# A streaming encoder step on one core: the MLP joins the attention's block, its first falling weights are prepared in the mix, the second queries are fetched in the projection's end, and the input stage is put in another order

## The reference, cut to what matters

```python
p = rms_norm(x, g_pre_mix) @ w_in            # 1024 x 5064: queries, keys, values, index queries, gates
o_a = window attention (128 keys, sinks)     # 16 heads of 64
o_b = attention over the 256 keys that an indexer picks
x1  = x + rms_norm((sig(g_a)*o_a + sig(g_b)*o_b) @ w_o, g_post_mix)
hid = square(relu(rms_norm(x1, g_pre_mlp) @ w_up))          # 1024 -> 4096
y   = x1 + rms_norm(hid @ w_down, g_post_mlp)               # 4096 -> 1024
```

## Time and profile before

| | us |
|---|---|
| three runs | 1955.41, 1956.94, 1957.11 |
| median | 1956.94 |
| the profiled execution | 1953.25 |
| its span, first to last instruction | 1951.5 |
| PE busy in it | 1877.9 (96%) |
| DVE, ACT, POOL busy | 1148.3, 711.1, 601.5 |
| mean granted TensorE clock | 0.990 of full |

### The profile page before, as it was taken

How to read it: one execution, slowest core, us unless ns; L and a number is a source line. 1 busy time by engine, 2 the same in 40 slices (tenths; PEclk the granted TensorE clock), 3 DMA queues, 4 the chain that set the end, 5 groups by cost and what they waited for, 6 DMA issues and landing times. The chain is left out here.

```text
span 1951.5 us, 32608 instructions
## 1 busy us (share of the span) xinstructions
PE 1877.9 (96%) x11780; PEld 1775.0 (91%) x11780; DVE 1148.3 (59%) x2732; ACT 711.1 (36%) x1420; POOL 601.5 (31%) x460
## 2 busy tenths in 40 slices
PE   5999999999997999999999999999999999999995
PEld 5889999877777999999998879999999999999995
DVE  5249999998665666676764654334333343344346
ACT  4335544223334555555564332222222222222212
POOL 2316544234233444444332012222222222222214
PEclk9999999999998999999999999999999999999998
DMA  5423333233438444444223313111111111111204
GB/s 174 126 66 103 93 92 86 87 102 99 105 98 185 106 99 100 99 99 89 67 66 109 118 54 109 43 43 48 43 48 43 43 43 43 43 43 43 64 1 162
DMA packets 180396, 160.23 MB, mean 82 GB/s; under 512 B 101472, under 2 KB 148432, under 8 KB 180288
## 3 DMA queue, kind: packets, MB, share of 16 engines
q1 hardware_dynamic: 166144, 140.32, 25.4%
q10 hardware_dynamic: 14144, 18.49, 4.0%
HBM read 120.63 MB, written 39.27 MB: 82 GB/s over the span
## 5 line engine op out<-in xcount | busy, mean ns | idle before, releaser
L2264 PE MATMUL ps<-hid_hi,weights 128*128 128x362 f32 (+1 forms) x1536 | 381.7, 328 | 3.9 <-POOL weights L2124 3.9
L1726 PE MATMUL ps<-x2T_hi,weights 128*128 128x362 f32 (+1 forms) x1536 | 378.2, 326 | 1.8 <-POOL weights L1858 1.5
L2264 PEld LDWEIGHTS ps<-hid_hi,weights 128*128 128x128 f32 x1536 | 271.9, 189 | 4.2 <-POOL weights L2124 4.2
L1726 PEld LDWEIGHTS ps<-x2T_hi,weights 128*128 128x128 f32 x1536 | 272.1, 188 | 2.4 <-POOL weights L1858 1.7
L2203 DVE TENSOR_TENSOR total<-total,ps 128x364 f32<-128x364 f32 (+1 forms) x360 | 189.1, 532 | 139.9 <-PE ps L2264 139.9
L1726 PE MATMUL ps<-x2T_lo,weights 128*128 128x362 f32 (+1 forms) x768 | 251.4, 327 | 0.0
L2264 PE MATMUL ps<-hid_lo,weights 128*128 128x362 f32 (+1 forms) x768 | 251.1, 327 | 0.0
L974 PE MATMUL ps<-xT_hi,w 128*128 128x362 f32 (+1 forms) x960 | 245.0, 329 | 1.6 <-PEq L165 1.6
L2188 DVE TENSOR_TENSOR hidden<-hidden 128x362 f32<-128x362 f32 (+1 forms) x96 | 53.9, 562 | 296.9 <-ACT hidden L2162 296.9
L2124 POOL TENSOR_TENSOR weights<-down_raw,weights 128x512 fp32r<-128x512 f32 x64 | 83.4, 1304 | 406.4 <-ACT weights L2153 406.4
L950 DVE MATCH_REPLACE8 score<-top,score 128x1024 f32<-128x1024 f32 (+5 forms) x208 | 198.6, 960 | 0.0
(11 more groups left out here) (189 smaller groups left out, 3205.8 us busy)
## 6 DMA issues: line engine op xcount, KB each, us to landing
q_raw<-q_scr SPq DMA_DIRECT2D x80, 256.0 KB, 5.1
w_raw<-in_w_in ACTq DMA_DIRECT2D x64, 256.0 KB, 3.0
up_raw<-in_w_up SPq DMA_DIRECT2D x64, 256.0 KB, 2.8
down_raw<-in_w_down SPq DMA_DIRECT2D x64, 256.0 KB, 2.6
gates<-gate_scr SPq DMA_DIRECT2D x34, 256.0 KB, 4.8
x_in<-in_x_prompt SPq DMA_DIRECT2D x16, 512.0 KB, 4.8
gate_scr<-stage SPq DMA_DIRECT2D x32, 256.0 KB, 3.0
q_scr<-stage SPq DMA_DIRECT2D x40, 181.0 KB, 3.1
```

The lines of the kernel that those rows point to most:

```text
L1726: last = pe.matmul(ps[:, bank, 0:n], a[:, k, fs], b, start=(k == 0 and i == 0), stop=(k == KT - 1 and i == 2))
L2264: more = pe.matmul(ps[:, UP_BANKS + g % DOWN_BANKS, 0:n], a[:, f, cols], h, start=(f == 0 and i == 0), stop=(f == FT - 1 and i == 2))
```

## The change

**Input stage.** SP's order of loads becomes x0, gain, units 2 and 3, x1, units 4 and 5, x2, units 6 and 7, x3, and then one next-chunk unit and one x tile in turn, with the stores begun inside that loop. ACT's queue loads units 0 and 1 alone. Units 4 to 7 get buffers of their own (`w_more`), so no load of the first chunk waits. All hi copies are ACT's; DVE has none. ACT runs a one-column square root (`warm`) first. PE's order is turn(t), group(t-1). The next chunk's units are spread over the tiles.
**Projection's end.** The four mask stores go ahead of the store of group 6. The first part of the banded values stays on SP behind that store, the second part (7 DMAs) goes to ACT's queue behind its evacuation of group 7. `load_q(1)` moves to SP behind the store of group 7. On POOL, `split_queries(1)` comes first in the attention, with a wait for the projection's last group; the small memsets (`LATE_SETS`), on which SP's sample values wait, come behind it. SP's attention begins with the distances, then the values of the other branch, then the gates.
**The MLP.** It loses its block: its five programs run behind the mix's. Its first four falling units are loaded by SP in the mix (before the store of tile 7, behind the turn of the last merged tile), copied by ACT between the two statistics of the last tile, and subtracted by POOL behind the rising units. Its first rising group waits for each unit k when it needs it. The final waits of SP move to the end.

```diff
 @@ input_norm, SyncE
+load_x(0)
+sp.dma_start(gain[:], g_pre_mix[0:1, :].to_broadcast([P, D])).then_inc(gains_loaded, 16)
+load_first(2)
+load_first(3)
+load_x(1)
+load_first(4)
+load_first(5)
+load_x(2)
+load_first(6)
+load_first(7)
+load_x(3)
+for t in range(X_IN, TILES):
+    load_next(KT + t - X_IN)
+    load_x(t)
+    if t >= X_IN + 2:
+        store(t - X_IN - 2)
+for t in range(TILES - X_IN - 2, TILES):
+    if KT + t + 2 < 2 * KT:
+        load_next(KT + t + 2)
+    store(t)
 @@ input_norm, ScalarE
-for k in range(RAW):
-    load_weight_unit(act, ws, w_raw, w_in, k)
+for k in range(2):
+    load_first_unit(act, ws, k, as_loaded(k), w_in)
 act.wait_ge(const_ready, 1)
+act.activation(warm[:], c["eps"][:], ACT.Sqrt)
+for t in range(2):
+    mean_square(t)
+    weights_hi(2 * t)
+    weights_hi(2 * t + 1)
+for t in range(TILES):
+    split_hi(t)
+    if t < 2:
+        weights_hi(4 + 2 * t)
+        weights_hi(5 + 2 * t)
+    if t + 2 < TILES:
+        mean_square(t + 2)
+    if t >= 2:
+        evacuate(t - 2)
+    if KT <= KT + t - 1 < 2 * KT and t >= 1:
+        weights_hi(KT + t - 1)
 @@ input_norm, VectorE
-for k in range(HI_BY_DVE):
-    dve.wait_ge(ws["loaded"][k % RAW], weight_loads(k))
-    dve.tensor_copy(w_hi[:, half_of(0), k, 0:T_WIDTH], w_raw[:, k % RAW, 0:T_WIDTH]).then_inc(ws["hi_dve"], 1)
 @@ input_norm, TensorE
-for t in range(TILES + 2):
+for t in range(TILES + 1):
     if t < TILES:
         turn(t)
-    if t >= 2:
-        group(t - 2)
+    if t >= 1:
+        group(t - 1)
 @@ projection, SyncE, last chunk
+if ch == LAST and g == VALUES_AT:
+    store_last_masks()
 store(ch, g)
 if ch == LAST and g == VALUES_AT:
-    load_values(0)
-if ch == LAST and g == VALUES_AT + 1:
-    load_values(1)
+    load_values()
+if ch == LAST and g == SECOND_AT:
+    load_second_queries()
 @@ projection, ScalarE, last chunk
+if ch == LAST and g == SECOND_AT:
+    load_more_values()
 @@ attention, SyncE
-sp.wait_ge(kv["mask_ready"], MASKS)
-for n in range(MASKS - SCORES, MASKS):
...
+for i in range(2):
+    load_dist(i)
 for dst, src in B_VALUES:
     sp.dma_start(dst, src).then_inc(b_values_loaded, 16)
-for n in range(MASKS - SCORES, MASKS):
-    sp.wait_ge(mask_stored[mask_slot(n)], 16 * (n // SCORES + 1))
-load_q(1)
-for i in range(2):
-    load_dist(i)
 @@ attention, GpSimd
     if s >= 2:
         pool.wait_ge(scored, CHUNK_BASE[SECTION_END[s - 2]])
+    else:
+        pool.wait_ge(ws["group_done"], PROJECTED)
...
+split_queries(1)
 for u in range(PROJECTED - STAGE, PROJECTED):
     pool.wait_ge(ws["stored"][u % STAGE], stage_stores(u))
 @@ output_mix, SyncE
+if t == TILES - 2:
+    sp.wait_ge(m_turned, 2 * TILES)
+    for u in range(DOWN_UNITS):
+        load_down_unit(sp, down, u, 0)
 sp.wait_ge(x1_ready, t + 1)
 @@ output_mix, GpSimd, behind the rising units
+for u in range(DOWN_UNITS):
+    pool.wait_ge(down["hi_done"], u + 1)
+    split_down_lo(pool, down, u)
 @@ output_mix, ScalarE
     norm_statistics(t - 1, 0, product(t - 1))
+    if t == TILES:
+        for u in range(DOWN_UNITS):
+            act.wait_ge(down["loaded"][u], 16)
+            split_down_hi(act, down, u)
 @@ early_up, TensorE
-pe.wait_ge(up["lo_done"], KT)
-up_product(pe, ps, x2T, up, g, EARLY_BANKS[g])
+up_product(pe, ps, x2T, up, g, EARLY_BANKS[g], weights_as_made=(g == 0))
 @@ up_product
+if weights_as_made:
+    pe.wait_ge(up["lo_done"], k + 1)
 @@ mlp, TensorE, first chunk
+pe.wait_ge(kv["mix_scaled"], TILES)
+pe.wait_ge(kv["x_lo_done"], 2 * TILES)
 @@ streaming_step
+raised = mlp(nc, top, c, x2T, ps, kv, up, down, a["g_post_mlp"], x1_scr, o["y_prompt"], o["y_sample"])
...
     mixed.tensor(pe)
+    raised.tensor(pe)
...
-mlp(nc, top, c, x2T, ps, weights, up, a["w_down"], a["g_post_mlp"], x1_scr, o["y_prompt"], o["y_sample"])
```

More of the change, by code:

```diff
@@ L2019, in mlp @@
         up_raw, up_loaded, up_src = up["raw"], up["loaded"], up["src"]
-        down_raw = sb("down_raw", [P, DOWN_UNITS, 512])
-        size = KT * CH
-        quarter = [weights[:, i * size:(i + 1) * size] for i in range(4)]
-        up_hi, up_lo = up["hi"], up["lo"]
-        down_hi, down_lo = (w.rearrange("p (k n) -> p k n", k=FT) for w in quarter[2:])
+        up_hi, up_lo, down_hi, down_lo = up["hi"], up["lo"], down["hi"], down["lo"]
+        x1_in = sb("x1_in", [P, 2, D])
         hidden = sb("hidden", [P, 2, 364])
@@ new lines, in gpsimd, with split_up_lo, all_down_lo @@
+        def gpsimd(pool):
+            def split_up_lo(j):
+                for k in range(KT):
+                    pool.wait_ge(up_hi_done, j * KT + (k + 1))
+                    pool.tensor_tensor(up_lo[:, k, :], up_raw[:, k // 2, k % 2, :], up_hi[:, k, :].bitcast(F32),
+                                       ALU.subtract).then_inc(up_lo_done, 1)
+            def all_down_lo(j):
+                for u in range(DOWN_UNITS):
+                    pool.wait_ge(down_hi_done, j * DOWN_UNITS + (u + 1))
+                    split_down_lo(pool, down, u)
+            with pool.Fori(0, N_CH - 1) as j:
+                split_up_lo(j + 1)
+                all_down_lo(j + 1)
+            pool.wait_ge(down_lo_done, N_CH * DOWN_UNITS)
+            for t in range(TILES):
+                r = tile_rows(t)
+                pool.wait_ge(scaled, t + 1)
+                pool.wait_ge(x1_loaded[t % 2], 16 * (t // 2 + 1))
+                pool.tensor_tensor(y[:r, t % 3, :], y[:r, t % 3, :], x1_in[:r, t % 2, :], ALU.add).then_inc(y_ready, 1)
+                pool.wait_ge(y_ready, t + 1)
@@ new lines, in scalar, with split_up_hi, chunk @@
+        def scalar(act):
+            def split_up_hi(j):
+                act.wait_ge(up_done, j * N_UP)
+                for k in range(KT):
+                    act.wait_ge(up_loaded[k // 2], (j + 1) * 16)
+                    act.activation(up_hi[:, k, :], up_raw[:, k // 2, k % 2, :], ACT.Copy).then_inc(up_hi_done, 1)
+            def chunk(j, first=False):
+                for g in range(N_UP + 1):
+                    if g < DOWN_UNITS and not first:
+                        act.wait_ge(down_done, j * N_DOWN)
+                        act.wait_ge(down_loaded[g], (j + 1) * 16)
+                        split_down_hi(act, down, g)
+                    if g < N_UP:
+                        n = UP_GROUPS[g][2]
+                        act.wait_ge(up_done, j * N_UP + (g + 1))
+                        if g >= 2:
+                            act.wait_ge(hid_lo_done, j * N_UP + (g - 1))
+                        elif not first:
+                            act.wait_ge(hid_lo_done, j * N_UP)
+                        act.activation(hidden[:, g % 2, 0:n], ps[:, up_bank(g, first), 0:n], ACT.Relu).then_inc(relu_done, 1)
+                    if g >= 1:
+                        f, t0, n = UP_GROUPS[g - 1]
+                        act.wait_ge(squared_done, j * N_UP + g)
+                        act.activation(hid_hi[:, f, t0:t0 + n], hidden[:, (g - 1) % 2, 0:n], ACT.Copy).then_inc(hid_hi_done, 1)
+            chunk(0, first=True)
+            with act.Fori(1, N_CH) as j:
+                split_up_hi(j)
+                chunk(j)
+            for t in range(TILES):
+                r = tile_rows(t)
+                act.wait_ge(y_turned, t + 1)
+                act.activation(squares[:r], y_banks(t), ACT.Square, accum_out=col["sum_sq"][:r, t:t + 1]).then_inc(sq_done, 1)
+                act.wait_ge(sq_done, t + 1)
+                act.activation(col["std"][:r, t:t + 1], col["sum_sq"][:r, t:t + 1], ACT.Sqrt, bias=c["eps"][:r, :],
+                               scale=1.0 / D).then_inc(std_ready, 1)
```

514 lines of the change are left out of this document (241 added, 273 removed).

## The result

The changed kernel takes 1938.9 us (median of 4 runs, 1937.0 to 1939.9), the kernel before 1956.4 beside it (4 runs, 1955.4 to 1957.1): ratio 0.9914, 95% interval 0.9903 to 0.9926. That is 17.5 us faster where 24.3 were forecast; 1938.9 lies inside the range, 6.3 us above the predicted time. The profiled execution took 1938.89 with a span of 1937.1, 14.4 us shorter than the span of before.

The account below looks back on a forecast made before the run. TensorE, busy 96% of the span, was taken as the bound, with its waits at three places to remove: 8.0 + 8.4 + 7.9 = 24.3 us, from the median 1956.94 to 1932.6 us; range 1925 to 1945.

Parts of the forecast that it names:

- the input stage: Kernel's start: first product group starts near 16.9 us instead of 25.88; gain 8.0 us, bounds 3 and 10.
- x1 as the deciding load: Input stage: the second tile decides when group 0 starts; x1 lands near 10 us, its `x_norm` is done at 14.8.
- rival (c): Input stage: loads sharing the DMA engines are the bound, not VectorE's queue; gain there 3 us, time 1937.6, chance 0.12.
- the MLP's start: Start of the MLP: waits for falling and rising weights and a half-clock stretch go; gain 7.9 us, or down to 6.
- the projection's end: Before attention section 1: the wait for second queries goes, less later values; net gain 8.4 us, bounds 4.7 and 9.8.
- I take 1.0: First value product, section 0: values delayed by the queries' 1 MB beside them cost 1.0 us, bounds 0 and 4.2.
- the 3.7 us of slack: Before section 1: second queries land at 582.7 and are split by 589.2, 3.7 us before they are needed.
- Rival (a): Projection's end gives its gain back, values and queries delaying each other; total gain 16.9 us, time 1940.0, chance 0.14.
- 0.5 us: Section 1's first six score matmuls: the slower run behind the idle gap goes, counted 0.5 us, bounds 0 to 0.9.
- The 8.9 us go: Between sections 0 and 1: TensorE's whole idle time for the second queries, 8.9 us, is gained.
- Rival (b): Section 0: GpSimd's split stops VectorE, 6.5 us of the middle gain go; time 1939.1, chance 0.04.
- Rival (d): ScalarE's last evacuation before attention is late behind seven value DMAs; slower kernel, 1962.7 at 5 us each, chance 0.02.

Follow-up runs that it names:

- experiment 2: The changed kernel with SyncE issuing the last four distance stores behind the eight value loads instead of ahead of them; 1937.3 us.
- experiment 5: The changed kernel with GpSimd's subtraction of the first queries waiting for VectorE's last mask but one; 1935.9 us (three runs).
- filled_gap: The changed kernel with 21 unused 128x208 products on TensorE ahead of the first value product's wait for the values; 1933.5 us.
- experiment 3: The change without its input stage (1943.4 us), without its second queries' part (1941.5 us), and the kernel before with the MLP's part alone (1945.3 us).
- mlp_part_alone: The kernel before with only the MLP's part of the change; 1945.3 us.
- 7: The changed kernel with distances and half the values on ScalarE ahead of group 7's evacuation, plus fillers (1930.5 us); also with further edits together (1929.7 us).
- all_four: The changed kernel with distances and half the values on ScalarE before group 7, GpSimd's subtraction behind the last mask but one, 12, 10 and 6 fillers; 1929.7 us.
- experiment 6: The changed kernel with 12 unused 128x512 products ahead of the first index scores, those of the sample tile; 1939.3 us.
- masks_on_act: The changed kernel with distances and half the values issued on ScalarE ahead of its evacuation of group 7, no fillers; 1935.7 us.
- no_input_part: The changed kernel with the input stage of the kernel before; 1943.4 us.
- masks_on_act_filled: The changed kernel with distances and half the values on ScalarE ahead of group 7's evacuation, 10 fillers before the first turn, 6 before the first value product; 1930.5 us.
- no_queries_part: The changed kernel with the projection's end of the kernel before; 1941.5 us.

## Why the prediction was right and wrong

**Right, the input stage** (8.0 against 7.3 at the stage's end). Group 0 behind the second tile, x1 as the deciding load, 2.0 us for a half-clock turn: all there. x1 was in ScalarE's hands at 10.05 and its root at 11.23, as reckoned; rival (c) did not occur. x1's `x_norm` ended at 15.41, not 14.8. What no term held is that some of this could be lost later, where TensorE next waits; by medians 4.5 us of it remain.

**Right, the MLP's start** (7.9 against 8.5 by profile). The waits for falling and rising weights are gone, the first falling stretch runs at full clock in 23.59 us, and ScalarE's late copies delayed nothing.

**Wrong, the projection's end** (8.4 against -0.7 by profile, some 3 by medians). Two steps failed.

The first is the term "I take 1.0" for the values, between the bounds 0 and 4.2, with the reason that half of them are ahead of all queries in SyncE's queue. It was 3.1. What is ahead of *them* in that queue was not counted: the distance stores had been moved in front of the store of group 6, with a wait for the last mask, and VectorE's meeting with GpSimd made that mask late. With the values ahead of them the wait was 0.6 (experiment 2), without the meeting 1.8 (5). The prediction said of the distances only that they land sooner. The queries' issue also took 6.29 us and not the 3.42 carried over from the earlier trace rows; they were split at 590.6, so the 3.7 us of slack were gone too, and at full clock section 1 would have waited 1.2 us. Rival (a) is this mechanism, priced at 1940.0, chance 0.14. That its price is near the measured 1938.9 is partly luck, since it has no term for the clock either. The Trainium skill, page "DMA: Bandwidth & Descriptors", section "Issuing engines are not separate DMA queues", says that two issuers share the 16 engines and only issue time is saved. The trace agrees: with both queues' values going out together it was 6.7 us from issue to landing in the median instead of 3.2. In filled_gap, where all but the last of SyncE's eight were issued ahead of ScalarE's seven (564.86 to 569.0, then 568.25 to 572.8), the median is 3.2 again and the longest 6.2: two issuers alone are not what made them slow, it was what was in flight at the time.

The second step that failed weighs more: no term had TensorE's clock in section 0. The profile of before showed it at 1.00 there and half clock only behind the 8.9 us gap, so 0.5 us was put down to it. The section's start has 1.4 us of idle time and small products, and is where the clock can fall in an execution; then it stays low to the section's end, 6.5 us. While TensorE waited for the queries behind it, that was hidden (experiment 3: at half clock mlp_part_alone's section 0 ended at 598.3, and its queries were split at 602.5). What makes the clock fall in one execution and not in the next stays open. "The 8.9 us go" was true as a wait and not as time.

**Rival (b) did not occur.** GpSimd's split ran beside section 0; VectorE and GpSimd in the changed kernel:
```profile
586.06 4.54 POOL L1511 TENSOR_TENSOR q_st<-q_raw,q_st 64x2048 fp32r<-64x2048 f32 x1
...
587.30 0.49 DVE L1615 CUSTOM_DVE_ANT_0 probs<-ps,near_a,neg_sinks 128x208 f32<-128x208 f32 x1 [0.24 <-PE ps L1683]
```
A score step took 0.49 us, as in the earlier trace rows. But its mechanism did strike at a place that the prediction did not look at, the last masks (experiment 5). Rival (d), late evacuations, did not occur in the change: the seven issues took 4.68 us, none over 0.83, and the last evacuation was at 573.29, right behind its product. With eleven issues in 7 it was group 7's evacuation that came late, and next to harmlessly.

The total was inside the range because rivals of this kind reached to 1945; that it lay only 6.3 us off is in part luck. By profile 14.4 us came and not 24.3, and 3.1 of the 17.5 by medians stand in no part of the two profiles. all_four brings 25.4, near the sum of 24.3, but with other edits than those forecast.

## What to carry to other kernels

A wait that is removed may have been hiding something that the profile of before doesn't show as a cost; ask what the stretch ahead of it takes at TensorE's half clock before its length is counted as gain. When a transfer is moved forward in a queue, look at what the moved block waits for and who now stands behind it. Where TensorE starts a stage of small products with gaps, a few products into a bank that is not yet in use, put in gaps that wait for others and not for TensorE itself, can be worth more than the gaps. Look in the timeline where they ran: those of experiment 6 stood 45 us ahead of the gap that they were meant for.

## What was not expected of the hardware

- By its times and mean granted clocks, one and the same kernel runs section 0 at either clock: masks_on_act took 1929.2 once and 1935.1 to 1936.7 three times, no_input_part 1936.4 once and 1943.3 to 1944.5 three times. With fillers at the section's start, filled_gap, masks_on_act_filled and all_four spread by 1.9, 2.5 and 0.8 us, and all twelve runs have a mean granted clock of 0.993 to 0.995, as the two fast runs above (0.994, 0.995); the six others of those two kernels have 0.988 to 0.990.
- VectorE's tensor_scalar of 128x384 in SBUF takes 0.36 us in seven profiles, and 2.96 to 4.75 in the seven where GpSimd's 4.6 us subtraction had begun before it. Score steps with PSUM input (0.49) and max8 of 128x512 in SBUF (0.69, in filled_gap beside the subtraction and in the changed kernel without it) are not touched. The Trainium skill, page "SBUF — State Buffer", section "SBUF: two separate sides", narrows what the prediction quoted from its "Terms": VectorE needs the shared ports only in its 2-port mode or with two SBUF inputs, and then whoever starts first keeps them for the whole instruction. The trace agrees: it was held only when GpSimd had begun, and then to GpSimd's end. (No run shows in which mode it ran.) `x_norm` has two SBUF inputs, and its 0.85 us in the prediction are such a wait too: in the changed kernel x1's began at 13.27, GpSimd's running operation ended at 14.3, and `x_norm` took 2.14 us, not 1.28; GpSimd's next then took 2.14 us, not 1.14. By these rows each engine in turn waited for the other.
- DMA issues were longer where the DMA engines were busier: the four query loads took 6.29 us to issue in the changed kernel (DMA share 1.25 from 574 to 580 us) and 3.19 in no_queries_part (0.79 from 580 to 584).
